# Second layer's attention taken in head pairs between the query, key and value projections of a two-block transformer kernel

## The reference, cut to what matters

```python
def _sb_attend(qs, qpos, kvs, kpos):
    z = jnp.einsum('bqhd,bkhd->bhqk', q, k).astype(jnp.float32) * (HEAD_DIM ** -0.5)
    mask = kpos[None, :] < qpos[:, None]
    log_keep = jnp.where(mask, jax.nn.log_sigmoid(-z), 0.0)
    later = lax.cumsum(log_keep, axis=3, reverse=True) - log_keep
    a = jnp.where(mask, jnp.exp(jax.nn.log_sigmoid(z) + later), 0.0)
    return jnp.einsum('bhqk,bkhd->bqhd', a.astype(v.dtype), v)
def sb_mixer(h, w_qkv, w_o):
    qkv = (h @ w_qkv).reshape(B, L, 3, N_HEADS, HEAD_DIM)
    ...
    return o.reshape(B, L, N_HEADS * HEAD_DIM) @ w_o
```

## Time and profile before

| | |
|---|---|
| median of 3 runs | 1098.32 us (1097.35 to 1098.92) |
| span of the profiled execution | 1096.2 us |
| TensorE matmul busy | 1037.4 us, 95% |
| VectorE, ScalarE, GpSimd busy | 799.4, 494.6, 176.5 us |
| chain that ended last, by engine | TensorE 83%, VectorE 11%, ScalarE 2% |

### The profile page before, as it was taken

The page is one execution under the profiler, slowest core; times in us unless marked ns, Lnnn a source line. Parts: engine busy times, 40 slices in busy tenths (PEclk is TensorE's granted clock), DMA queues, the critical chain, the costliest instruction groups (busy, mean ns, idle before and its releaser), DMA issues.

```text
span 1096.2 us, 20849 instructions
## 1 busy us (share of the span) xinstructions
PE 1037.4 (95%) x7740; PEld 958.2 (87%) x7740; DVE 799.4 (73%) x1305; ACT 494.6 (45%) x750; POOL 176.5 (16%) x179
## 2 busy tenths in 40 slices
PE   6579999999999999999999999999998999999995
PEld 3279999999998579999999887999556999999995
DVE  6979888788997679876667846663755877676554
ACT  3155444344434454545444422566443455554442
POOL 2550000012000028200035302000311060000011
PEclk9789999999999999999999999999999999999998
DMA  6248767566784035555445532543102355554452
GB/s 219 77 154 285 267 252 267 198 234 241 276 324 173 1 116 212 194 189 191 154 143 201 176 116 77 192 168 139 30 29 87 117 191 192 191 178 158 162 186 83
DMA packets 35802, 187.51 MB, mean 171 GB/s; under 512 B 4168, under 2 KB 7657, under 8 KB 21097
## 3 DMA queue, kind: packets, MB, share of 16 engines
q1 hardware_dynamic: 35752, 186.85, 48.1%
HBM read 185.78 MB, written 1.05 MB: 170 GB/s over the span
## 4 chain that ended last, share of the span: by engine, by line
PE 83%; DVE 11%; ACT 2%; issue 1%; DMA 1%; SPq 1%; POOL 0%; DVEq 0%; ACTq 0%; POOLq 0%
PE ps L368 24%; PE ps L370 24%; PE ps L369 24%; DVE wl L316 3%; PE ps L1730 1%; DMA sini<-in_sini 1%; PE ps L1743 1%; PE ps L1568 1%; PE ps L1598 1%; DVE dump L1136 1%; ACT wh L310 1%; PE ps L1625 1%; PE ps L1624 1%; DVE xl L1116 1%; PE ps L1709 1%
## 5 line engine op out<-in xcount | busy, mean ns | idle before, releaser
L368 PE MATMUL ps<-xh,wh 128*128 128x256 f32 (+3 forms) x1808 | 520.0, 288 | 9.6 <-DVE xl L1116 5.5
L370 PE MATMUL ps<-xl,wh 128*128 128x256 f32 (+3 forms) x1808 | 520.2, 288 | 0.0
L369 PE MATMUL ps<-xh,wl 128*128 128x256 f32 (+3 forms) x1808 | 518.2, 287 | 0.0
L316 DVE TENSOR_TENSOR wl<-stage,wh 128x1024 fp32r<-128x1024 f32 (+2 forms) x320 | 365.4, 1153 | 144.0 <-ACT wh L310 139.8
L310 ACT ACTIVATE wh<-stage 128x1024 fp32r<-128x1024 f32 (+2 forms) x320 | 307.2, 970 | 242.7 <-PE ps L370 188.2
L368 PEld LDWEIGHTS ps<-xh,wh 128*128 128x128 f32 x1808 | 343.5, 190 | 14.9 <-DVE xl L1116 7.0
L369 PEld LDWEIGHTS ps<-xh,wl 128*128 128x128 f32 x1808 | 343.6, 190 | 1.6
L370 PEld LDWEIGHTS ps<-xl,wh 128*128 128x128 f32 x1808 | 341.8, 189 | 1.4
L368 PE MATMUL ps<-gh,wh 128*128 128x256 f32 (+1 forms) x528 | 150.3, 285 | 2.9 <-DVE wl L316 1.5
L369 PE MATMUL ps<-gh,wl 128*128 128x256 f32 (+1 forms) x528 | 149.5, 283 | 0.0
L370 PE MATMUL ps<-gl,wh 128*128 128x256 f32 (+1 forms) x528 | 149.1, 282 | 0.0
(11 more groups left out here) (234 smaller groups left out, 898.5 us busy)
## 6 DMA issues: line engine op xcount, KB each, us to landing
stage<-in_w_gu SPq DMA_DIRECT2D x66, 1024.0 KB, 4.8
stage<-in_w_dn SPq DMA_DIRECT2D x48, 704.0 KB, 4.0
adaw<-in_w_ada SPq DMA_DIRECT2D x48, 512.0 KB, 4.9
stage<-in_w_gates SPq DMA_DIRECT2D x8, 1024.0 KB, 4.7
stage<-in_w_q SPq DMA_DIRECT2D x6, 1024.0 KB, 5.0
stage<-in_w_k SPq DMA_DIRECT2D x6, 1024.0 KB, 4.8
stage<-in_w_v SPq DMA_DIRECT2D x6, 1024.0 KB, 6.8
stage<-in_w_hy SPq DMA_DIRECT2D x6, 1024.0 KB, 4.8
```

What stands on the lines that cost most here:

```text
L316: nc.vector.tensor_tensor(wl[:, b, w], stage[:, b, w], wh[:, b, w].bitcast(fp32), ALU.subtract).then_inc(split_lo, 1)
L368: nc.tensor.matmul(psum, wh[:, b, w], xhi, start=first and n == 0, stop=False)
L369: nc.tensor.matmul(psum, wl[:, b, w], xhi, start=False, stop=False)
L370: last = nc.tensor.matmul(psum, wh[:, b, w], xlo, start=False, stop=close and n == len(blocks) - 1)
```

## The change

q1, k1 and v1 become one stage `qkv` of 12 chunks whose 24 tiles come in the order q, k, v of each head pair. The three products of a pair go to three PSUM banks, and the attention of the pair before stands between them, both heads in one instruction wherever shapes allow: sigmoids over 832 columns, one scan over 832 with zeroes between the four parts, products and copies over both heads, the 16 meta keys of both heads in one transpose and one product. The last attention steps stand between parts of o1's first four tiles, which are left one block short until the last output is there. Each tile of qkv is loaded by a DMA of its own.

The modulation tiles leave q1, k1, v1: 22 stay in gu0, 8 in dn0, 4 in o1, and 14 go to gu1, of which the 8 with two vectors take one per pair of chunks (`modulate_first` with the first chunk, `modulate_second` with the second) and the last 6 one per chunk. In o1 and in gu1 the load of a modulation tile now stands behind the load of the chunk in whose work it is used.

```diff
-    ("pool", 2, 8), ("gu0", KF, 16), ("dn0", 16, 11), ("q1", 4, 16), ("k1", 4, 16), ("v1", 4, 16),
+    ("pool", 2, 8), ("gu0", KF, 16), ("dn0", 16, 11), ("qkv", 12, 16),
...
-ADA_AT = {"gu0": (0, 22), "dn0": (22, 8), "q1": (30, 4), "k1": (34, 4), "v1": (38, 4), "o1": (42, 4), "gu1": (46, 2)}
+ADA_AT = {"gu0": (0, 22), "dn0": (22, 8), "o1": (30, 4)}
...
             sp.wait_ge(res, KD + RES0["dn0"])
-            sp.dma_start(sel[:, :], A["sel"]).then_inc(sel_in, 16)
+            for lo, n in ((0, TM), (TM, P + META), (SC, TM), (SC + TM, P + META)):
+                sp.dma_start(sel[:, lo:lo + n], A["sel"][:, 0:n]).then_inc(sel_in, 16)
+            for c in range(2, 4):
+                load_qkv(c)
             sp.dma_start(hc[:, :, :], A["ctx"].rearrange("p (k t) -> p k t", k=KD)).then_inc(ctx_in, 16)
-            chunks_ada("v1")
-            chunks_ada("o1")
-            chunks_ada("gu1", 0, 2)
-            with sp.Fori(2, KF // 2) as g:
+            for c in range(4, NCHUNK["qkv"]):
+                load_qkv(c)
+            with sp.Fori(0, NCHUNK["o1"] // 2) as g:
+                for b in range(2):
+                    load_chunk("o1", g + PAIR0["o1"], b)
+                    ada(2 * g + (ADA_AT["o1"][0] + b), b)
+
+            with sp.Fori(0, 4) as t:
+                for u in range(2):
+                    for b in range(2):
+                        load_chunk("gu1", 2 * t + (PAIR0["gu1"] + u), b)
+                    ada(2 * t + (SC1 + u), u)
+            with sp.Fori(8, KF // 2) as g:
                 for b in range(2):
                     load_chunk("gu1", g + PAIR0["gu1"], b)
+                    ada(2 * g + (G2B - 16 + b), b)
...
+                z = banks[:, 3:5, 0:SC]
+                act.activation(keep[:, 1:2 * SC + 1].rearrange("p (h x) -> p h x", h=2), z, ACT.Sigmoid, scale=-1.0)
+                act.activation(take[:, :].rearrange("p (h x) -> p h x", h=2), z, ACT.Sigmoid).then_inc(soft_ready, 1)
...
+            for i in range(KD + 1):
+                if i < KD:
+                    ahead_of(3 * i, hi_part)
+                if i >= 2:
+                    out_hi(i - 2)
+                if i >= 1:
+                    value_tokens(i - 1)
+                    sigmoids_of(i - 1)
+                if i < KD:
+                    ahead_of(3 * i + 1, hi_part)
+                    ahead_of(3 * i + 2, hi_part)
+                if i >= 1:
+                    turned_back(i - 1)
...
+            def weights(p):
...
+                link(dve.tensor_tensor_scan(out=left[:, :], data0=keep[:, 0:2 * SC], data1=sel[:, :],
+                                            initial=0.0, op0=ALU.mult, op1=ALU.add))
...
+            def score(p):
...
+                for lo, hi, tokens in ((0, TM, slice(0, P)), (TM, SC, slice(P, TX))):
+                    for h2 in range(2):
+                        o = HD * h2
+                        ins = pe.matmul(ps[3 + h2][:, lo:hi], q1[o:o + HD, p, tokens],
+                                        k1[o:o + HD, p, tokens.start:TM], start=True, stop=True)
...
+            for i in range(KD):
+                qkv_tile(3 * i)
+                if i == 0:
+                    norm_sum("dn0", TM)
+                if i >= 2:
+                    attend(i - 2)
+                if i >= 1:
+                    score(i - 1)
+                    turn_values(i - 1)
+                qkv_tile(3 * i + 1)
+                qkv_tile(3 * i + 2)
+                if i >= 1:
+                    turn(i - 1)
+            attend(KD - 2)
+            score(KD - 1)
+            turn_values(KD - 1)
...
+            o1_part(0, 0, KD - 1)
+            o1_part(1, 0, KD - 1)
+            turn(KD - 1)
...
+            o1_part(2, 0, KD - 1)
+            attend(KD - 1)
...
+            o1_part(3, 0, KD - 1)
+            pe.wait_ge(o_lo, KD)
+            for m in range(4):
+                o1_part(m, KD - 1, KD)
```

More of the change, by code:

```diff
@@ L230, in build @@
         yim = vxc[:, 2:4, :]
-        ps = [ctx.enter_context(nc.psum_tensor(f"ps{i}", [P, BANK], fp32)) for i in range(8)]
+        banks = ctx.enter_context(nc.psum_tensor("ps", [P, 8, BANK], fp32))
+        ps = [banks[:, i, :] for i in range(8)]
         fin = gates[:, :, 0, :]
@@ L270, in build @@
         at = 0
-        for s in ("gu0", "q1", "k1", "v1", "gu1", "k2", "v2", "q2", "hy", "gu2"):
+        for s in ("gu0", "gu1", "k2", "v2", "q2", "hy", "gu2"):
             free[s], free0[s], grows[s] = drained, at, 1
@@ L844, in _, with ahead_of @@
-            for hh in range(HEADS):
-                if 1 <= hh < HEADS - 1:
-                    sigmoids_of(hh + 1, (hh + 1) % 2)
-                if hh:
-                    wide_back(hh - 1, (hh - 1) % 2, hh < 3)
-                if hh % 2 and hh >= 3:
-                    out_hi((hh - 3) // 2)
-            wide_back(HEADS - 1, 1)
+            def ahead_of(n, part):
+                at = n + 4
+                s = "qkv" if at < 24 else "o1"
+                part(s, PAIR0["qkv"] + at // 4, at // 2 % 2, at % 2)
@@ L1245, in _ @@
             dve.wait_ge(cvec_ready, 1)
[L1246 removed]
+            hidden_stage(0, TM)
             down_stage("dn0", TM, "mix1", ADA_AT["dn0"][0], 0)
             inverse_root("attn", TM, 6)
[L1252 to L1265 removed]
@@ L1305, in _ @@
[L1305 to L1312 removed]
+            for i in range(KD + 1):
+                if i < KD:
+                    read_tile(3 * i)
+                    ahead_of(3 * i, lo_part)
+                if i >= 2:
+                    out_lo(i - 2)
+                if i == 1:
+                    dve.wait_ge(sel_in, 16 * 4)
+                if i >= 1:
+                    weights(i - 1)
+                if i < KD:
+                    read_tile(3 * i + 1)
+                    ahead_of(3 * i + 1, lo_part)
+                    read_tile(3 * i + 2)
+                    ahead_of(3 * i + 2, lo_part)
@@ L1642, in _, with qkv_tile @@
-            pe.wait_ge(v_act, 4)
-            pe.wait_ge(v_dve, 2)
-            for hh in range(HEADS):
-                turn(hh)
-                if hh + 2 < HEADS:
-                    score(hh + 2)
-                if hh:
-                    attend(hh - 1)
-            attend(HEADS - 1)
-            two_tiles("o1", wide(ALT, TX), TX, None, (o_lo, 1))
+            def qkv_tile(n):
+                q, b, j, kind = PAIR0["qkv"] + n // 4, n // 2 % 2, n % 2, n % 3
+                width = TX if kind == 0 else TM
+                before = [m for m in range(n) if QKV_BANK(m) == QKV_BANK(n)]
+                if before:
+                    pe.wait_ge(qkv_read, before[-1] + 1)
+                if kind == 2 and n >= 3:
+                    pe.wait_ge(v_act, n // 3)
+                pe.wait_ge(split_lo, 4 * PAIR0["qkv"] + n + 1)
+                products(ps[QKV_BANK(n)][:, 0:width], b, range(8 * j, 8 * j + 8), wide(0, width),
+                         k_wait=(nlo, IN0["dn0"] + 1) if n == 0 else None).then_inc(used, 1)
@@ new lines, in _, with o1_part @@
+            score(KD - 1)
+            turn_values(KD - 1)
+            o_in = wide(ALT, TX)
+            def o1_part(m, k0, k1, at=0):
+                b, j = m // 2, m % 2
+                if k0 == 0:
+                    pe.wait_ge(split_lo, 4 * PAIR0["o1"] + m + 1)
+                    pe.wait_ge(o_lo, KD - 2)
+                if k1 == KD - 1:
+                    pe.wait_ge(o_lo, KD - 1)
+                ins = products(ps[m][:, 0:TX], b, range(8 * j + k0, 8 * j + k1), o_in[k0:k1],
+                               first=k0 == 0, close=k1 == KD)
+                if k1 == KD:
+                    ins.then_inc(used, 1)
```

351 lines of the change are left out of this document (185 added, 166 removed).

## The result

The changed kernel takes 1136.33 us (median of 4 runs, 1132.59 to 1142.09) against 1098.62 for the one before it beside it: a ratio of 1.0355, 95% interval 1.0319 to 1.0391, slower by 37.7 us. Its profiled span is 1132.8 us, 36.6 above that of before.

What follows compares the result with a forecast made beforehand. It took TensorE to bound projections, attention and gu1. Terms -15.5 + 19.7 + 0.4 + 30.4 + 0.4 = +35.4 on a span of 1096.2 gave 1131.6; with 2.1 from span to median, forecast 1133 us, range 1112 to 1148.

Steps and rivals of the forecast that it cites:

- both rings: Modulation loads waiting in SyncE's queue hold weight loads behind them: o1 into gu1's start +19.7 us, gu1's last six chunks +30.4.
- Attention, -15.5: Attention among the projections: paired heads side by side on TensorE, 33.6 + 3.5 = 37.1 us for 52.55; from -20 to -11.
- The turns' waits: TensorE's waits for a pair's other work: 1.4 us over all pairs, first table load 1.3, last pair 0.8.
- The hold in o1, +19.7: A waiting modulation load delays o1's fourth load, the next one gu1's first two: +19.7 us, from 15 to 23.
- attention's gain alone: Rival: the held loads cost nothing, so only the shorter attention shows: 1083 us, down to 1078; chance 0.10.
- gu1's body, +0.4: One reduce and copy per gu1 chunk hides on VectorE, 5.4 us under TensorE's 5.69; +0.4 us, 0 to 6.
- The ring in gu1's last chunks, +30.4: From gu1's chunk 16 on, loads wait for reduces: 11.75 us a chunk for 5.69; +30.4 us, from 22 to 35.
- the landing: Time from issue to arrival of a 1 MB weight load behind 0.5 MB of modulation: 4.8 + 1.4 = 6.2 us.
- Clock, +0.4: TensorE may restart at half rate after the new waits of 5 to 8 us: +0.4 with two added copies, at most 5.
- One ring only: Rival: load and reduce overlap more, so gu1's tail runs near pace and only o1's delay remains: 1107 us; chance 0.06.
- Heads apart: Rival: alternating row halves drain TensorE, 1.8 us a pair come back, attention gains nothing: 1148 us; chance 0.08.
- Slower by clock: Rival: TensorE at half rate through both rings and into dn1, +8 us: 1141 us; chance 0.07.

Runs made afterwards that it cites:

- the released kernel: The changed kernel with each modulation tile of o1 and gu1 loaded behind the chunk two later than the one using it: 1087.56 us, ratio 0.9877 to the kernel before.

## Why the prediction was right, and where it wasn't

The forecast was 1133 and the time is 1136.3, with the sign, both rings and their places as told. Term by term:

**Attention, -15.5; measured -18.3.** Right in mechanism: the heads run side by side (0.91 us for both heads' scores; taken apart, +1.1 a pair). A pair costs 3.85 us instead of the 4.2 that I summed, 2.8 us in all, which is this term's miss. The term mis-sized is the one without a row of its own, 0.6 a pair for entering and leaving fp32 passes: 0.27 is what the trace leaves for it; transposes were 1.09 for 1.2, outputs 1.58 for 1.51. The turns' waits came as a sum: forecast 1.4 over all, a table load 1.3 and a last pair 0.8, 3.5; measured nothing in the middle pairs, 1.47 in the first, 1.27 and 0.62 in the last, 3.4. (The eight tiles of q1 have 256 columns and not 272 as the prediction says, in both kernels, so nothing rests on it.) By the rule of the Trainium skill against it ("TensorE: Matmul & The Clock Gate", Part 3) weight loads overlap running matmuls only where the row group differs. It would have given outputs 0.94 longer a pair; the outputs took 1.58 us for the 1.51 forecast, so the trace doesn't agree with it here.

**The hold in o1, +19.7; measured +20.9, but the hold is only two thirds of it.** The path was worked out whole and came true. VectorE uses o1's first tile at 389.67 us; 7.0 later the modulation load is released (396.67; forecast 7.0), 15.7 later the fourth chunk starts (15.6), 30.2 later gu1 (28.5, its load landed 1.2 later than forecast), and `norm_sum` comes 39.1 after T (37.9). What failed is the name of the term: I took 18.2, the step in the kernel before, as what it would be without the hold. VectorE's chain of 26 us had its first 7.6 us hidden under o1's first tiles; now 0.8. Without the hold the step takes 25.7 us: 13.4 are the hold, 7.5 are the lost cover. A sum over the held path gives the right total whatever the other path is, and says nothing about what removing the hold will bring; so I expected 1082 of the released kernel, and "attention's gain alone" at 1083 as a rival. Their mechanism occurred, at 1087.6.

**gu1's body, +0.4.** With both holds released, the step from `norm_sum` behind o1 to the one behind dn1 takes 190.3 us for 190.5 before: a reduce a chunk is hidden. Right.

**The ring in gu1's last chunks, +30.4; measured +34.3, and +31.2 for the ring alone.** A turn took 12.6 us where I had 11.75. The term that was mis-sized is the landing: 6.2, from a rate seen once, against 5.4 to 5.9 and 7.4 to 8.2 in turns. The steps around the turns were sized well. Starts of chunk 21, of dn1, of its second half-sum, and a product further on:

```profile
570.39 0.38 PE L384 MATMUL ps<-xh,wh 128*128 128x256 f32 x1 [2.97 <-DVE up_t L1224]
...
581.24 0.36 PE L384 MATMUL ps<-gh,wh 128*128 128x256 f32 x1 [2.95 <-DVE wl L332]
...
588.49 0.39 PE L384 MATMUL ps<-gh,wh 128*128 128x256 f32 x1 [1.60 <-DVE gl L1239]
...
595.40 0.42 PE L384 MATMUL ps<-gh,wh 128*128 128x256 f32 x1
```

dn1 comes 10.85 us after chunk 21, 5.2 late (forecast 10.5 and 4.8), its second half-sum 7.25 after that, for 3.9 of work at full rate: 3.4 late (4.2). The waits in the rows are shorter than these delays because TensorE spent the rest of them at half rate, 16 products behind 571.4 and 16 behind 581.7.

**Clock, +0.4.** The rows show 0.78 in o1 and 0.87 in the ring. Behind the waits of 5.5 and 6.0 us the products go at half rate, 0.21 us, from the first one on; behind that of 1.78 us twelve go at 0.118 and then some 15 at 0.21:

```profile
393.96 0.42 PE L384 MATMUL ps<-xh,wh 128*128 128x256 f32 x1
394.17 0.42 PE L385 MATMUL ps<-xh,wl 128*128 128x256 f32 x1
```

and so also without the hold, from 392.8. In o1 and in the ring TensorE then waits for data again, and no cost shows. Where nothing waits behind, it does: 15 products at half rate from 595.40 on, in dn1, are 1.4 us, a little over what I had, and the 11 in the released kernel's gu1 are 1.2. The Trainium skill ("TensorE: Matmul & The Clock Gate", Part 1) states that the throttled rate is the default and that activity releases it. At the two long waits the trace agrees, 0.21 us a product from the first on; at the wait of 1.78 us the first twelve products are at full rate.

**The sum.** -18.3 for -15.5, +20.9 for +19.7, +34.3 for +30.8 (both terms of gu1): three misses of 2.8, 1.2 and 3.5 us, the first against the other two, and the unchanged stretches +1.6 and -1.9. That the total is right to 3 us is in part luck: the terms are each off by 1 to 4 and the signs cancel.

**The rivals.** One ring only decides at a turn of 5.7 us; the turn was 12.6. Heads apart: with the scores one head after the other the stage is 7 us longer, and as changed they run in 0.91. Slower by clock: the half rate did run through both rings and into dn1, as this rival has it, but only some 1.4 us of it show outside the waits, for its 8.

## What to carry to other kernels

In a queue that issues both prefetches and rarely used operands, a wait holds everything behind it: ask of each wait which work it names, and whether the loads behind it are needed by that same work or the next chunk. If so it closes a ring, whose turn (release, landing, splits, reduce) replaces the chunk's time, here 12.6 us for 5.7, and one chunk of slack removes it whole. And where tiles that ended one by one end together, the engine behind them loses the time between them as cover: look where its chain begins, and cost the stage on every engine without the suspected stall too, since the old time of the stage isn't its floor.

## What the runs showed of the hardware

- Two heads' fp32 products on the two halves of the array run fully side by side for scores (row halves: eight in 0.91 us, four apart in 0.89).
- A ring through one DMA queue has a landing that alternates between 5.2 to 6.3 and 7.2 to 8.3 us for the same 1 MB behind the same 0.5 MB, in two stages; behind 0.06 MB it is 4.8 to 5.1 throughout. Why is open.
- A wait of 1.8 us ahead of o1's third chunk, the same in all ten kernels with the new attention, was followed by some 15 products at 0.21 us instead of 0.118 in five of them and by none in the other five. A short wait can be followed by half rate; what decides is open.
- From `norm_sum` behind dn1 to the next one in the second block, the same instructions in all kernels, took 281.2 to 286.5 us from profile to profile. In one stretch of it the granted clock was 0.91 in the longest and 0.98 in the released kernel. A difference of 5 us there need not come from an edit elsewhere; look at the marks ahead of it.
